# Leaving out 48 unused matrix products on TensorE: 36 where layer 1 begins, 12 in the expert routing

## The reference, cut to what matters

```
for i in range(2):
    h = rms_norm(x, mix_norm_g[i])
    proj = h @ w_in[i]                      # SSD, gating, attention and gate columns
    x = x + (sum of three gated branches of proj) @ w_out[i]
    h = rms_norm(x, ffn_norm_g[i])
    if i == 0: x = x + (silu(h @ wg) * (h @ wu)) @ wd          # dense, width 2816
    else:      x = x + moe_ffn(h, router_w, wg, wu, wd)        # top 2 of 8 experts, width 3584
```

## Time and profile before

| | before |
|---|---|
| median of three runs | 1979.59 us |
| the profiled execution | 1978.6 us, its span 1976.4 us |
| TensorE busy | 1935.4 us, 98% of the span, 9504 products |
| VectorE busy | 1523.4 us, 77% |
| ScalarE busy | 1261.4 us, 64% |
| mean granted TensorE clock over the span | 0.996 of full |
| DMA | 497.83 MB, mean 252 GB/s |

### The profile page before, as it was taken

One profiled execution on the slowest core, in us unless ns is written; L12 is line 12 of the kernel. 1 busy time (PEld: TensorE's weight loads), 2 busy tenths in 40 slices (PEclk: granted clock), 3 DMA queues, 4 the chain that ended last, 5 costly groups with the idle time before them and its releaser, 6 DMA issues.

```text
span 1976.4 us, 24178 instructions
## 1 busy us (share of the span) xinstructions
PE 1935.4 (98%) x9504; PEld 1604.9 (81%) x9504; DVE 1523.4 (77%) x1908; ACT 1261.4 (64%) x1597; POOL 1.2 (0%) x9
## 2 busy tenths in 40 slices
PE   6999999999999999999899999999999999999998
PEld 6788888778889688888788888888888888888787
DVE  6777666654458767665698998989989899898897
ACT  5756574544346655664477776777767777677775
POOL 0000000000000000000000000000000000000000
PEclk9999999999999999999899999999999999999999
DMA  6445334455354435247599999999999999999891
GB/s 225 158 138 170 129 110 154 173 190 184 132 202 137 165 128 170 86 167 274 198 375 348 344 377 338 359 354 341 374 338 360 352 340 377 340 356 366 314 373 58
DMA packets 220036, 497.83 MB, mean 252 GB/s; under 512 B 8630, under 2 KB 14996, under 8 KB 219668
## 3 DMA queue, kind: packets, MB, share of 16 engines
q1 hardware_dynamic: 219924, 496.29, 70.2%
HBM read 495.22 MB, written 1.05 MB: 251 GB/s over the span
## 4 chain that ended last, share of the span: by engine, by line
PE 76%; DVE 3%; ACT 1%; issue 0%; POOLq 0%; DVEq 0%; PEldq 0%
PE ps L940 12%; PE ps L942 12%; PE ps L941 12%; PE ps L931 6%; PE ps L933 6%; PE ps L932 6%; PE ps L1001 4%; PE ps L1002 4%; PE ps L1003 4%; PE ps L1299 2%; PE ps L911 2%; PE ps L1311 1%; PE ps L887 1%; DVE w_lo L1742 1%; PE ps L1070 1%; PE ps L1068 1%
## 5 line engine op out<-in xcount | busy, mean ns | idle before, releaser
L1742 DVE TENSOR_TENSOR w_lo<-piece,w_hi 128x1024 fp32r<-128x1024 f32 (+1 forms) x742 | 855.2, 1215 | 85.0 <-ACT w_hi L1362 84.6
L1362 ACT ACTIVATE w_hi<-piece 128x1024 fp32r<-128x1024 f32 (+1 forms) x742 | 731.8, 1048 | 74.7 <-PE ps L933 37.8
L940 PE MATMUL ps<-w_hi,xg_hi 128*128 128x512 f32 x896 | 354.8, 396 | 3.4 <-POOLq L841 1.8
L942 PE MATMUL ps<-w_hi,xg_lo 128*128 128x512 f32 x896 | 349.9, 391 | 0.0
L941 PE MATMUL ps<-w_lo,xg_hi 128*128 128x512 f32 x896 | 349.4, 390 | 0.0
L1806 DVE TENSOR_TENSOR w_lo<-piece,mixer_hi 128x1024 fp32r<-128x1024 f32 (+1 forms) x192 | 229.1, 1215 | 105.8 <-ACT mixer_hi L1416 105.3
L1416 ACT ACTIVATE mixer_hi<-piece 128x1024 fp32r<-128x1024 f32 (+1 forms) x192 | 198.6, 1050 | 142.4 <-PE ps L1003 117.0
L931 PE MATMUL ps<-w_hi,hid_hi 128*128 128x512 f32 x536 | 209.4, 391 | 1.5 <-DVE hid_lo L1782 1.5
L933 PE MATMUL ps<-w_hi,hid_lo 128*128 128x512 f32 x536 | 208.8, 390 | 0.0
L932 PE MATMUL ps<-w_lo,hid_hi 128*128 128x512 f32 x536 | 208.5, 389 | 0.0
L940 PEld LDWEIGHTS ps<-w_hi,xg_hi 128*128 128x128 f32 x896 | 168.9, 188 | 37.9 <-issue 2.2
(11 more groups left out here) (288 smaller groups left out, 2435.2 us busy)
## 6 DMA issues: line engine op xcount, KB each, us to landing
piece<-in_moe_w_gate SPq DMA_DIRECT2D x56, 2048.0 KB, 8.4
piece<-in_moe_w_up SPq DMA_DIRECT2D x56, 2048.0 KB, 8.4
piece<-in_moe_w_down SPq DMA_DIRECT2D x56, 2048.0 KB, 8.6
piece<-in_w_in SPq DMA_DIRECT2D x30, 2048.0 KB, 9.4
piece<-in_ffn_w_gate SPq DMA_DIRECT2D x5, 2048.0 KB, 7.8
piece<-in_ffn_w_up SPq DMA_DIRECT2D x5, 2048.0 KB, 7.8
piece<-in_ffn_w_down SPq DMA_DIRECT2D x5, 2048.0 KB, 8.1
piece<-in_w_br_ssd SPq DMA_DIRECT2D x4, 2048.0 KB, 8.6
```

Of the source, the lines that this page charges most:

```text
L940: pe.matmul(b, a_hi, hi[:, cs_], start=(kk == 0), stop=False)
L942: last = pe.matmul(b, a_lo, hi[:, cs_], start=False, stop=(kk == KD - 1))
L1362: act.activation(hi, slots[s][:, at_:at_ + n], ACT.Copy).then_inc(S["hi_made"], 1)
L1742: dve.tensor_tensor(w_lo[s][:, at_:at_ + n], slots[s][:, at_:at_ + n], hi.bitcast(F32), ALU.subtract).then_inc(S["lo_made"], 1)
```

## The change

The helper and its three calls go, and with the third call the wait ahead of it. Nothing else is touched; on the other engines every instruction stands where it stood.

```diff
-            def stay_awake(n, a, b):
-
-                for _ in range(n):
-                    pe.matmul(ps[:, b], a[:, 0:P], a[:, 0:N], start=True, stop=True)
...
                 done(pe.transpose(bank("vec")[:, 0:P], vec[:, :], ident))
 
-                if L:
-                    stay_awake(20, hT_hi[:].rearrange("p k n -> p (k n)"), bank_of("ht00"))
                 for t in range(NT):
                     passed(pe, "normed", t + 1)
                     for hh in range(2):
                         turn_over(f"ht{t}{hh}", [xn[:, t, c * P:(c + 1) * P] for c in range(4 * hh, 4 * hh + 4)])
-                if L:
-                    stay_awake(16, yT_hi[:].rearrange("p k n -> p (k n)"), bank_of("xbc0"))
                 passed(pe, "h_lo_made", 4)
...
             last.then_inc(S["logits"], 1)
-            pe.wait_ge(S["lo_made"], DENSE_ADDS["lo_made"] + 2)
-            stay_awake(12, w_hi[:, 0, :], 5)
             pe.wait_ge(S["chosen"], 1)
```

## The result

| | before | after |
|---|---|---|
| median of 20 runs each | 1979.39 us (1976.94 to 1981.86) | 1983.3 us (1981.2 to 1986.34) |
| ratio after to before, 95% interval | | 1.0020 (1.0013 to 1.0027) |
| the profiled execution, its span | 1978.6 us, 1976.4 us | 1985.7 us, 1983.5 us |

What follows compares the result with a forecast made beforehand. TensorE was taken as the bound, with no slack behind either place of change. Terms 1.15 + 1.9 - 0.4 + 0.4 = +3.05 us on a 1979.6 us median gave 1982.7 us; range 1981.3 to 1984.1, 8 in 10 1980.0 to 1985.6.

Steps and rivals of the forecast that it cites:

- Layer 1, place in the queue: At layer 1's start both groups of removed products lie wholly in waits, so taking them out frees 0 us.
- Transposes: Layer 1's 16 transposes run at the lower clock as in layer 0, so the first projection begins 1.15 us later.
- First projection: Layer 1's first projection runs 3.5 to 5.1 us at the lower clock: +1.9 us, between 1.6 and 2.3.
- The price of 0.446 us: In the first projection each microsecond at the lower clock loses 0.446 us, from product spacings of 0.118 and 0.213 us.
- The ranks: In the routing, without the 12 products ahead of them, the ranks let VectorE go on earlier: -0.4 us.
- The gather and what follows: In the routing the gather runs slow for longer: +0.4 us, between 0 and 0.8, passed on to L911.
- the same again behind L911: At the first expert's start, the low clock already costs about 2.3 us; the same cost was expected after the change.
- The sum: Over the whole kernel the terms add to +3.05 us, likeliest a small loss that reads as no change.
- The first rival: The routing pays as well: the gather meets the lower clock to its end; +5.3 us in all, 1984.9 us; chance 0.29.
- The gap does lower the clock: Rival denied this at layer 1: no loss there, the routing saves 0.4 us, 1979.2 us; chance 0.10.
- The 12 products are not shown to be harmful: Rival said they were, in the routing: clock stays high from the logits on; -2.7 us, 1976.9 us; chance 0.04.
- the three earlier falls: Clock falls at 946, about 956.2 and 976.7 us, with pauses of 1.0 to 3.81 us, cited for layer 1's gap.

Runs made afterwards that it cites:

- a1: The changed kernel executed once more, nothing else changed; 1981.88 us.
- a3: The changed kernel executed once more, a fourth look, nothing else changed; 1981.64 us.
- e1: Kernel before with only layer 1's 36 unused products (20 and 16) left out, the routing's 12 kept; 1983.58 us, ratio 1.0019.
- e3: Kernel before with only the 20 products ahead of layer 1's transposes left out; 1981.1 us, ratio 1.0005.
- a2: The changed kernel executed once more, a third look, nothing else changed; 1982.47 us.
- e4: Kernel before with only the 16 products behind layer 1's transposes left out; 1982.61 us, ratio 1.0015.
- e2: Kernel before with only the routing's 12 products between logits and ranks left out; 1979.09 us, ratio 1.0001.
- b2: Kernel before plus 4 unused products ahead of the second logits batch and 4 between the ranks and the gather; 1976.56 us, ratio 0.9984.
- b3: Kernel before plus unused products at layer 0's start, in the first expert's wait and in the routing, all together; 1970.83 us, ratio 0.9959.
- b4: b3 with 20 in place of 12 unused products behind layer 0's transposes; 1970.35 us, ratio 0.9948 to the kernel before.
- b1: Kernel before plus 14 unused products in the 3.81 us wait ahead of the first expert's first transposes; 1978.01 us, ratio 0.9991.

## Why the prediction was right, point by point

**What bounds the kernel.** That a microsecond lost at layer 1's start reaches the end whole holds: from the cumulative sums to the logits every profile has 302.0 to 302.2 us, however late the stage began.

**Layer 1, place in the queue: 0.** Right. With both groups out nothing began earlier.

**Transposes: +1.15 us.** Right to the hundredth, in after, a1 to a3, e1 and e3. Taking layer 0 as the copy of what layer 1 would become was the step that gave it; 1.71 us, the difference of the transposes' own durations, would have been too much.

**First projection: +1.9 us (1.6 to 2.3).** Right. In the three executions without the slower pace B is longer by 2.15, 1.77 and 2.18 us, 2.03 in the mean; in the first profile by 3.14, of which 1.28 are the slower pace and 1.86 the clock. The price of 0.446 us for each microsecond at the low clock can be tested, as the clock's return is seen in windows of one microsecond, here of a1, a2, a3 and e4:

```profile
591.00:592.00 1.00, 1.00 (x10) 0.98 0.00 0
```

```profile
591.00:592.00 1.00, 1.00 (x9) 0.77 0.00 0
```

```profile
590.00:591.00 1.00, 1.00 (x7) 0.63 0.00 0
```

```profile
590.00:591.00 1.00, 1.00 (x8) 0.63 0.00 0
```

The low clock lasts 4.2 us of the projection in after, and 4.8, 3.9, 4.8 and 5.9 us in a1, a2, a3 and e4. Times 0.446 that is 1.87, 2.1, 1.75, 2.1 and 2.6 us; B is longer by 1.86 (without the slower pace), 2.15, 1.77, 2.18 and 2.66. The Trainium skill's rule for the penalty ("TensorE: Matmul & The Clock Gate", "Terms"), one half of the slow time, would give an estimated 2.1, 2.4, 2.0, 2.4 and 3.0 us. It is above the measured loss each time, and the measured ratio decides.

**The ranks: -0.4 us.** Right, -0.43 us in the first profile.

**The gather and what follows: +0.4 us (0 to 0.8), and the same again behind L911.** In the four executions (after, a1, a2, a3) D is longer by 1.12, 0.37, 0.09 and 0.31 us, 0.47 in the mean. The 1.12 lies above the range given, and so does the gather's 6.57 us, where 5.4 to 6.3 was the sign named; in a1 to a3 it took 5.5 to 5.8. The 1.12 came together with an earlier return of the clock behind L906 (E shorter by 1.08 us), so that C to E sum to 129.88, 130.17, 129.90 and 130.18 us against 130.24 before. The routing as a whole gave back 0.2 us in the mean where I had 0.0. That two small terms of opposite sign cancel was the forecast; that they did so within 0.2 us is partly luck, as e2's single profile, with the same routing code, has them at -2.5.

**The sum.** A to E is longer by 3.93, 3.24, 2.58 and 3.27 us in the four executions, 3.26 in the mean; 3.05 was forecast, and the timed runs have 3.9 with 2.6 to 5.3. The mean of the four contains the slower pace once, which is 0.3 us of it. What the timed runs have beyond that is within their interval, and I leave it there. I had expected the loss to read as no change; with 20 executions of each kernel it doesn't, since the interval leaves no change out.

**The rivals.** The first rival's +5.3 us lies at the edge of what the timed runs allow, so the traces decide: the routing does not pay as well, as C to E are not longer in any of after and a1 to a3. The gap does lower the clock. The 12 products are not shown to be harmful: in e1, where the low clock held while most of them ran, they took 5.32 us and C rose by 1.08 us, but E was 1.02 us shorter, and C to E sum to 130.31 us against 130.24. What the prediction lacked is the two accidents. They make 1.3 and 1.6 us of difference between executions of one kernel, and two of the first kind and one of the second stood in the one profile after, so that it alone would have told of a loss of 7 us.

**A premise that did not hold.** The prediction takes the fall at 946 us as one behind 8-column products and a pause of 1.0 us. Between the two batches of logits TensorE also transposes eight tiles of x, 1.07 us of work, right ahead of that pause. The two rows are of the kernel before and of the one after:

```profile
943.87 1.07 PE L887 MATMUL ps<-const,x 128*128 128x128 f32 x8
```

```profile
949.59 1.37 PE L882 MATMUL ps<-const,x 128*128 128x128 f32 x8
```

In the profile after the clock fell at 950.2 us, while those transposes still ran (they took 1.37 us) and before the pause began at 951.0; in e2 it fell only in the second batch. So the pause by itself isn't what lowers it there, and the three earlier falls were weaker evidence for the one in the gap of 5.8 us than they looked. The stronger evidence was layer 0, and the fall came.

## What to carry to other kernels

Products without a use can be worth their place if they stand wholly in a wait and the work behind them is bound by TensorE: here 36 of them were worth 3 to 4 us, and 8 to 10 us more lay in putting others into waits, and between small steps, that had none. Price each group by what starts next at full clock, and look at one execution's other stages before you put a difference of a few microseconds down to the change. A copy of the same steps elsewhere in the trace, run at the other level of the clock, was the best price list here.

## What the runs showed of the hardware that was not expected

- A stream of 128x256 products at full granted clock ran at either 0.118 or 0.122 us a product, from start to start, for all of the 288 products of the first projection (some 35 us), without a wait and in one and the same kernel (87 or 84 in 10 us).
- Between the two batches of logits (16 instructions of 8 columns each) TensorE has eight transposes and a pause of 1.0 us. In the eleven profiles with nothing else there the clock fell between these transposes and the middle of the second batch, which then took up to 3.56 us; with four products of 512 columns in the pause (0.92 us) it did not fall, and the batch took 1.92 us (b2, b3 and b4).
- Sixteen transposes at the low clock, 3.7 us of continuous work, can be followed by the clock's return or not. In e3 it came back 0.2 us behind their end, with one or two products of 512 columns begun. In layer 0 of e2, e3 and b1 nothing but one transpose near 9.8 us and those sixteen, all at the slow pace, ran before the fall that the traces record at 19.6 to 19.9 us, so the clock had come back behind them, at 16.0 us or later. In layer 1 of after, e1 and a1 to a3 it had not come back when the projection began 4.4 us behind them.
- A return that came too early was of no use: in layer 0 of e2, e3 and b1 the clock fell again ahead of the first projection, which then ran at the low level until 26.4 to 26.7 us (until 24.4 in the kernel before), and the stage took 57.7 to 57.8 us in place of 56.65.
